# DeltaNet scan, before and after: 16x16 blocks turned on VectorE by 0/1 columns, DRAM scratch laid out by half of the partitions, 15 transfers per pair of steps in place of 36

## The reference, cut to what matters

```python
lmat = jnp.where(strict, jnp.einsum('bhnik,bhnjk->bhnij', k_beta, k) * decay, 0.0)
tmat = triangular_solve(eye + lmat, eye, left_side=True, lower=True, unit_diagonal=True)
u = tmat @ v_beta
w = tmat @ (k_beta * exp(g))
intra = where(incl, (q @ k^T) * decay, 0.0)
def step(S, xs):
    v_new = u_c - w_c @ S
    o_c = q_c @ S + a_c @ v_new
    S = S * exp(gl_c) + k_c^T @ v_new
```

## Time and profile before

| | us |
|---|---|
| median of three runs | 2504.52 |
| the profiled execution: its own time | 2506.25 |
| the profiled execution: its span | 2504.3 |
| PE busy in the span | 2159.4 (86%) |
| DVE, ACT, POOL busy | 906.5, 682.8, 266.2 |
| DMA queue of SP and ACT: share of 16 engines | 20.5% |

### The profile page before, as it was taken

One profiled execution on the slowest core, in us unless ns is written; L12 is line 12 of the kernel. 1 busy time (PEld: TensorE's weight loads), 2 busy tenths in 40 slices (PEclk: granted clock), 3 DMA queues, 4 the chain that ended last, 5 costly groups with the idle time before them and its releaser, 6 DMA issues. The chain is left out here.

```text
span 2504.3 us, 39485 instructions
## 1 busy us (share of the span) xinstructions
PE 2159.4 (86%) x16431; PEld 1329.9 (53%) x16431; DVE 906.5 (36%) x1760; ACT 682.8 (27%) x1386; POOL 266.2 (11%) x381
## 2 busy tenths in 40 slices
PE   4987999989997587888897999999999699799960
PEld 3545676665553477877753555555455444344420
DVE  3254666634883355455551011010223300000116
ACT  6122666643441232332220000000111122122223
POOL 2000000000000444433100000000000000000013
PEclk8998999999998698999898999999999699999985
DMA  9324000010100232323203111120313455776225
GB/s 331 130 88 121 4 4 1 2 43 26 30 0 1 43 63 46 62 43 58 57 0 92 26 34 43 25 67 1 136 60 117 150 185 179 250 239 214 85 101 201
DMA packets 240544, 210.12 MB, mean 84 GB/s; under 512 B 130348, under 2 KB 202352, under 8 KB 239728
## 3 DMA queue, kind: packets, MB, share of 16 engines
q1 hardware_dynamic: 223632, 152.93, 20.5%
q0 software_dynamic: 11696, 36.31, 4.9%
q10 hardware_dynamic: 5040, 18.35, 1.8%
HBM read 165.37 MB, written 42.01 MB: 83 GB/s over the span
## 5 line engine op out<-in xcount | busy, mean ns | idle before, releaser
L741 PE MATMUL ps<-R 128*128 128x512 f32 (+1 forms) x816 | 301.2, 530 | 11.3 <-SPq L525 8.4
L1008 PE MATMUL ps<-R 128*128 128x512 f32 (+1 forms) x768 | 286.1, 526 | 19.9 <-DMA R<-in_w_dn_br_dram 17.8
L1084 PE MATMUL ps<-R 128*128 x560 | 260.1, 619 | 25.7 <-SPq L653 22.5
L900 PE MATMUL ps<-R 64*64 64x64 f32 x5120 | 181.7, 230 | 67.8 <-ACT R L1280 30.5
L741 PEld LDWEIGHTS ps<-R 128*128 128x128 f32 x816 | 158.6, 195 | 150.7 <-issue 132.8
L1008 PEld LDWEIGHTS ps<-R 128*128 128x128 f32 x768 | 147.2, 192 | 152.3 <-issue 144.9
L900 PEld LDWEIGHTS ps<-R 64*64 64x64 f32 x5120 | 172.0, 145 | 87.4 <-ACT R L1280 37.4
L1084 PEld LDWEIGHTS ps<-R 128*128 128x128 f32 x560 | 110.7, 199 | 169.6 <-issue 169.6
L1753 DVE TENSOR_TENSOR R<-ps,R 128x512 f32<-128x512 f32 (+1 forms) x48 | 28.9, 603 | 394.1 <-ACT R L1353 393.3
L1920 DVE COPY R<-ps 128x256 f32<-128x256 f32 x35 | 14.9, 425 | 383.4 <-PE ps L1109 383.4
L2071 POOL DMA_INDIRECT R<-h_scratch,slot_i x35 | 33.0, 942 | 1124.6 <-DVE slot_i L1903 749.6
(11 more groups left out here) (265 smaller groups left out, 2700.0 us busy)
## 6 DMA issues: line engine op xcount, KB each, us to landing
R<-in_w_mod_dram SPq DMA_DIRECT2D x12, 2048.0 KB, 9.1
slot_output<-R ACTq DMA_DIRECT2D x35, 512.0 KB, 3.6
R<-in_w_gate_e_dram SPq DMA_DIRECT2D x16, 1024.0 KB, 6.8
R<-in_w_up_e_dram SPq DMA_DIRECT2D x16, 1024.0 KB, 10.2
R<-in_w_down_e_dram SPq DMA_DIRECT2D x16, 1024.0 KB, 12.0
R<-in_w_in_dram SPq DMA_DIRECT2D x30, 512.0 KB, 5.4
R<-tu_scratch SPq DMA_DIRECT2D x160, 64.0 KB, 2.6
R<-in_x_sample_dram SPq DMA_DIRECT2D x16, 512.0 KB, 6.0
```

The lines of the kernel that those rows point to most:

```text
L741: last = mm(ps[:, u % 4, 0:w], w_sb[n % NW][:, k, :], hT[:, k, c0:c0 + w], start=(k == 0), stop=(k == KD - 1))
L900: last = mm(ps[lo, bank, a * C:(a + 1) * C], lhs(a)[lo], rhs(a)[lo], start=start and (alone or a == 0), stop=stop and (alone or a == PAIRS ...
L1008: mm(ps[:, o + x, 0:w], wk[:, x, k, :], hT[:, k, c0:c0 + w], start=(k == 0), stop=(k == KD - 1))
L1084: last = mm(ps[:, 2 + t % 2, :], hsT[t % 2][:, k, :], R[:, bass.ds(at + (RB + k * 512), 512)], start=(k == 0), stop=(k == KD - 1))
```

## The change

Per pair of steps POOL writes L with 2 transfers a step in place of 4 (both directions in one, 64x8x64). SP reads all 128 blocks with one transfer in place of 4. The scratch `tu_scratch` is laid out so that both directions and two steps lie together; SP writes it with 2 transfers in place of 8 and reads it with 4 a step in place of 8. No byte more or less is moved, and the pieces keep their sizes (64 bytes in the block transfers, 256 bytes in the planes).

Transposing goes from ACT to DVE. A constant `block_dir` has two columns of 0 and 1 that tell by partition which direction a block is of. DVE makes `b_turn = b_in * dir0 + b_in^T * dir1` with two instructions ahead of the substitution, and two more each for the matrix `b_t` (the inverse for direction 0, the transposed one for direction 1) and for `b_u` (the other way) behind it. `b_t` is the buffer `b_in`. The semaphores `bt_turned` and `base_turned` and the two ACT instructions are gone. SP's loop runs over pairs; the context state is stored two pairs later than before, behind the planes of pair 4.

The diff, cut:

```diff
-    parts = [np.eye(P), same, np.ones((P, P))] + upto + after_bd + level + [eye, -eye, rot, before]
+    parts = [np.eye(P), same, np.ones((P, P))] + upto + after_bd + level + [eye, -eye, rot, before, (part[:, None] // 16) % 2 == np.arange(2)[None, :]]
...
-        tu_d = nc.dram_tensor("tu_scratch", [4, 2, P, 16 * PLANE // P], F32).ap()
+        tu_d = nc.dram_tensor("tu_scratch", [2, 4, P, 16 * PLANE // P], F32).ap()
...
-        b_in, b_turn, b_inv, b_invt = [scr(256, "R1").rearrange("p (r c) -> p r c", r=16) for _ in range(4)]
+        b_in, b_turn, b_inv, b_u = [scr(256, "R1").rearrange("p (r c) -> p r c", r=16) for _ in range(4)]
+        b_t = b_in
...
-        def planes_of(x, n, d, h):
-            return bass.AP(x.tensor, (16 * n + 8 * d + 4 * h) * PLANE, [[C, C], [PLANE, 4], [1, C]])
+        def planes_of(x, n, h):
+            return bass.AP(x.tensor, (16 * n + 8 * h) * PLANE, [[C, C], [PLANE, 8], [1, C]])
+
+        def blocks_of(x, n):
+            return bass.AP(x.tensor, 16 * n * PLANE, [[16 * C + 16, P], [C, 16], [1, 16]])
...
             def inverses_back(b):
                 sp.wait_ge(S["base_done"], b + 1)
-                sp.wait_ge(S["base_turned"], b + 1)
                 for s in (2 * b, 2 * b + 1):
                     if s - 4 >= 0:
-                        sp.wait_ge(S[f"tu_in{(s - 4) % 3}"], landed(s - 4, 3, 8))
-                    for d in range(2):
-                        for x in range(2):
-                            src = b_inv if x == d else b_invt
-                            sp.dma_start(blocks_of(tu_d, 2 * (s % 4) + x, d), src[block_rows(s, d)]).then_inc(S["tu_out"], 16)
-                sp.wait_ge(S["tu_out"], 128 * (b + 1))
+                        sp.wait_ge(S[f"tu_in{(s - 4) % 3}"], landed(s - 4, 3, 4))
+                for x, src in enumerate((b_t, b_u)):
+                    sp.dma_start(blocks_of(tu_d, 4 * x + 2 * (b % 2)), src).then_inc(S["tu_out"], 16)
+                sp.wait_ge(S["tu_out"], 32 * (b + 1))
                 for s in (2 * b, 2 * b + 1):
                     if s - 2 > 0:
                         sp.wait_ge(S["vn_mm"], s - 2)
                     for x in range(2):
-                        for d in range(2):
-                            for h in range(2):
-                                sp.dma_start(tu[s % 3][h * C:(h + 1) * C, x, 4 * d:4 * d + 4], planes_of(tu_d, 2 * (s % 4) + x, d, h)).then_inc(S[f"tu_in{s % 3}"], 16)
-
-            for s in range(NCK):
-                sp.wait_ge(S["lt_out"], 64 * (s + 1))
-                if s % 2 == 0 and s > 0:
-                    inverses_back(s // 2 - 1)
-                if s // 2 > 0:
-                    sp.wait_ge(S["base_done"], s // 2)
-                    sp.wait_ge(S["bt_turned"], s // 2)
-                for d in range(2):
-                    sp.dma_start((b_turn, b_in)[d][block_rows(s, d)], blocks_of(lt_d, s, d)).then_inc(S["bt_in"], 16)
-                if s == CTX_CH + 2:
+                        for h in range(2):
+                            sp.dma_start(tu[s % 3][h * C:(h + 1) * C, x], planes_of(tu_d, 4 * x + s % 4, h)).then_inc(S[f"tu_in{s % 3}"], 16)
+
+            for b in range(NCK // 2):
+                sp.wait_ge(S["lt_out"], 64 * (b + 1))
+                if b > 0:
+                    sp.wait_ge(S["base_done"], b)
+                sp.dma_start(b_in, blocks_of(lt_d, 2 * b)).then_inc(S["bt_in"], 16)
+                inverses_back(b)
...
-            inverses_back(NCK // 2 - 1)
...
-                if n >= 2 and n % 2 == 0 and n // 2 - 1 < NCK // 2:
-                    b = n // 2 - 1
-                    act.wait_ge(S["bt_in"], 64 * (b + 1))
-                    if b > 0:
-                        act.wait_ge(S["base_done"], b)
-                    f(b_turn[C:2 * C].rearrange("p r c -> p c r"), b_in[C:2 * C], ACT.Copy).then_inc(S["bt_turned"], 1)
...
-                if n >= 2 and n % 2 == 0 and n // 2 - 1 < NCK // 2:
-                    b = n // 2 - 1
-                    act.wait_ge(S["base_done"], b + 1)
-                    if b > 0:
-                        act.wait_ge(S["tu_out"], 128 * b)
-                    f(b_invt.rearrange("p r c -> p c r"), b_inv, ACT.Copy).then_inc(S["base_turned"], 1)
...
-                signal = "base_done" if i == 15 else "dve_chain"
-                v.tensor_reduce(b_inv[:, i, 0:i], tmp, AX.X, ALU.add, negate=True).then_inc(S[signal], 1)
-                dve.wait_ge(S[signal], count(signal))
+                v.tensor_reduce(b_inv[:, i, 0:i], tmp, AX.X, ALU.add, negate=True).then_inc(S["dve_chain"], 1)
+                dve.wait_ge(S["dve_chain"], count("dve_chain"))
             def base(b, first, end):
                 if first == 1:
-                    dve.wait_ge(S["bt_in"], 64 * (b + 1))
-                    dve.wait_ge(S["bt_turned"], b + 1)
-                    if b > 0:
-                        dve.wait_ge(S["base_turned"], b)
-                        dve.wait_ge(S["tu_out"], 128 * b)
+                    dve.wait_ge(S["bt_in"], 16 * (b + 1))
+                    v.tensor_scalar(b_turn, b_in, block_dir[:, 0:1], None, ALU.mult).then_inc(S["dve_chain"], 1)
+                    dve.wait_ge(S["dve_chain"], count("dve_chain"))
+                    v.scalar_tensor_tensor(b_turn, b_in.rearrange("p r c -> p c r"), block_dir[:, 1:2], b_turn, ALU.mult, ALU.add).then_inc(S["dve_chain"], 1)
+                    dve.wait_ge(S["dve_chain"], count("dve_chain"))
                 for i in range(first, end):
                     substitute(b, i)
+                if end == 16:
+                    if b > 0:
+                        dve.wait_ge(S["tu_out"], 32 * b)
+                    for x, dst in enumerate((b_t, b_u)):
+                        v.tensor_scalar(dst, b_inv, block_dir[:, x:x + 1], None, ALU.mult).then_inc(S["dve_chain"], 1)
+                        dve.wait_ge(S["dve_chain"], count("dve_chain"))
+                        signal = "base_done" if x else "dve_chain"
+                        v.scalar_tensor_tensor(dst, b_inv.rearrange("p r c -> p c r"), block_dir[:, 1 - x:2 - x], dst, ALU.mult, ALU.add).then_inc(S[signal], 1)
+                        dve.wait_ge(S[signal], count(signal))
...
-                        pool.wait_ge(S["lt_out"], 64 * (n - 1))
-                    for d in range(2):
-                        for h in range(2):
-                            pool.dma_start(planes_of(lt_d, n - 1, d, h), la[(n - 1) % RING][h * C:(h + 1) * C, 1, 4 * d:4 * d + 4]).then_inc(S["lt_out"], 16)
+                        pool.wait_ge(S["lt_out"], 32 * (n - 1))
+                    for h in range(2):
+                        pool.dma_start(planes_of(lt_d, n - 1, h), la[(n - 1) % RING][h * C:(h + 1) * C, 1]).then_inc(S["lt_out"], 16)
```

More of the change, by code:

```diff
@@ L129, in build @@
         levels = take(2 * 2 * C).rearrange("p (l d c) -> p l d c", l=2, d=2)
-        eye_st, neg_eye, rot, before = take(C), take(C), take(P), take(P)
+        eye_st, neg_eye, rot, before, block_dir = take(C), take(C), take(P), take(P), take(2)
         small = sb("small", [P, small_np.shape[1]])
@@ L183, in build @@
           ot_used  pad_zeroed
-          gm_ready decay_mm e_ready gr_ready e_masked el_ready kd_ready qd_ready gram_mm la_ready lt_out bt_in bt_turned
-          base_done base_turned tu_out x4_mm x4_ready t4_mm t4_ready u4_mm u4_ready x5_mm x5_ready u5_mm u5_ready
+          gm_ready decay_mm e_ready gr_ready e_masked el_ready kd_ready qd_ready gram_mm la_ready lt_out bt_in
+          base_done tu_out x4_mm x4_ready t4_mm t4_ready u4_mm u4_ready x5_mm x5_ready u5_mm u5_ready
           kt_mm kdec_ready r_mm r_ready vn_mm vn_ready kv_mm s_ready qs_mm av_mm o_used
@@ L556, in inverses_back @@
                     for x in range(2):
[L557 to L570 removed]
+                        for h in range(2):
[6 more added lines that the diff above has]
+                inverses_back(b)
+                if b == CTX_CH:
                     sp.wait_ge(S["s_ready"], PAIRS * CTX_CH)
@@ L912, in _ @@
                 if now:
-                    pe.wait_ge(S[f"tu_in{s % 3}"], landed(s, 3, 8))
+                    pe.wait_ge(S[f"tu_in{s % 3}"], landed(s, 3, 4))
                     pe.wait_ge(S["la_ready"], s + 1)
@@ L1720, in _ @@
                         dve.wait_ge(S["av_mm"], s)
-                        dve.wait_ge(S["lt_out"], 64 * s)
+                        dve.wait_ge(S["lt_out"], 32 * s)
                     v.tensor_tensor(la[n % RING].rearrange("p x a c -> p a x c"), ps[:, 0:2, :].rearrange("p b (a x c) -> p (b a) x c", a=4, x=2),
@@ L1982, in _ @@
                 for x in range(2):
-                    pool.dma_start(tu_d[i, x], zero_f).then_inc(S["pool_dma"], 16)
+                    pool.dma_start(tu_d[x, i], zero_f).then_inc(S["pool_dma"], 16)
             pool.wait_ge(S["pool_dma"], 128)
```

5 lines of the change are left out of this document (removed).

## The result

The changed kernel takes 2488.63 us (median of five runs, 2484.59 to 2492.22), the kernel before 2502.87 beside it: ratio 0.994, 95% interval 0.9927 to 0.9953, 14.2 us less. Run again later beside the kernel before it took 2494.19 against 2501.29 (0.9966, 0.9951 to 0.9982), so its gain lies between 7 and 14 us, where 34.8 were forecast. The time lies in the range that was stated (2452 to 2492), but the sum behind it came out otherwise. All medians here are of executions in the faster of the chip's two states; one of e5's six, with 4598.7 us, was not and is left out.

A forecast was written before the change was run, and what follows sets the result against it. PE was taken to be held in the scan by waits for ACT's copy, `tu` and DVE's mask. Terms 15.4 + 10.1 - 1.7 + 11 = 34.8 us off 2504.52 gave 2470 us, range 2452 to 2492.

The forecast's parts named there:

- What bounds the kernel now: PE waits in the scan: 29.8 us for ACT's copy, 21.7 for planes in `tu`, 14.9 for DVE's mask.
- SP and DMA: Fewer, larger transfers: writing phase 4.9 us, chain 10.6 for 15.7; `tu` waits 15.4 us less, first pair included.
- DVE, added: Turning instructions on DVE per pair: 1.0 us ahead of the first substitution row, 2.0 behind the last.
- odd waits: PE at the head of odd iterations: ACT's copy wait replaced by mask waits; with POOL's share 31.5 us, 1.7 more.
- The term of 0.3 us a pair: POOL's masking beside DVE's last substitution rows and new instructions slows DVE: 2.7 us in all.
- Late substitutions: SP free earlier for the next L, so the 14.9 us of mask waits go, less 4.8: 10.1 us gained.
- even waits: PE's waits in even iterations for the mask before `u5`, 14.9 us: forecast to fall by 10.1.
- The first substitution rows: 1.0 us more before the `x5` mask, cover just used up; 4.8 us of waits stick out.
- The clock: PE's slow stretches after four `tu` waits and two long mask waits go: 11 us come back.
- The rivals: Chain fits partly, 2491 (0.13); issues not the limit, 2504 (0.07); slower transfers, 2545 (0.05); more gained, below 2456 (0.09).
- the 2 us of the first pair: `tu` wait before the first pair: chain gains 5.1 us, new DVE instructions lose 3.0, 2 us net.

The follow-up runs named there:

- e5: The changed kernel with DVE's turning behind the substitution done twice over, 2.0 us more of DVE per pair: 2522.5 us.
- e9: The kernel before, 36 transfers, with ACT's turning behind the substitution moved behind the v_new copy and the decay exponentials: 2510.1 us.
- e1: The changed kernel with POOL's two writes of L issued first in its iteration, ahead of its kd and qd products: 2490.4 us.
- e3: The changed kernel without its six turning operations per pair, transfers left as they are: 2439.9 us.
- e8: The kernel before with SP's reads of L and writes of the blocks merged over the pair, 30 transfers, ACT turning: 2493.4 us.
- e14: The changed kernel without the two turning operations ahead of the substitution, the four behind it kept: 2480.7 us.
- e7: The kernel before with DVE turning as in the change, planes and 36 transfers as they were: 2523.2 us.
- e10: The kernel before with 18 transfers per pair through another order of the planes, ACT turning as before: 2481.4 us.
- e12: The kernel before with 18 transfers, ACT's turning moved behind the v_new copy and exponentials, and POOL writing L first: 2473.8 us.

## Why the prediction was wrong, point by point

**What bounds the kernel now** named the three places rightly, and e9 shows what it missed: they are one loop with two paths, DVE's string and the chain over DRAM, of nearly one length with 36 transfers. Taking 3 us off one only hands the wait to the other.

**SP and DMA**: right. 4.67 us of writing for 4.9, the chain 10.1 us (998.32 to 1003.02 + 3 x 0.755 + 3.1, the median landing of a read) for 10.6, and the waits for `tu` behind the first pair 1.7 us and, in the second profile, 0, where there were 13.5. Only the first pair fails: 9.5 us for 8.3, where I had it 2 us better. SP's first write there comes 3.9 us later than before, behind 3.4 us of turning, and the chain behind it is 4.4 us shorter; `x4` starts 0.5 us earlier, and PE had come to it 1.8 us earlier than before.

**DVE, added**: right for the pair alone (0.35 and 0.65 us, 1.04 together), low behind the substitution: 2.57 us for 2.0 from 995.75 on, since the first instruction stands beside POOL's (0.83 for 0.35). The odd waits came out at 34.2 us for 31.5, 2.7 more. The block between DVE and POOL is larger than the 0.4 of the earlier trace rows: 0.68 and 0.80 in e1. The term of 0.3 us a pair for it, 2.7 in all, was too small: with the six operations DVE is busy 237.1 us in the scan and without them 201.4 (e3), 35.7 more, where their own lengths (0.35 and 0.65) make 27. The other 9 us, 1.0 a pair, are instructions that took longer, and those seen to do so stand beside POOL's.

**The failed step is "Late substitutions"**: it said that SP is free in time, that DVE never waits for L and that 10.1 us are gained in the even iterations. The even waits rose instead, from 14.9 us to 21.1 (18.8 in the second profile), and DVE waited for L eight times, 10.4 us. That step asked when SP is free, not when both halves of L are written; POOL's L2023 at 1012.54 sets it, and the merged read, which could be issued only at the later of two events, moved from 3.8 to 5.1 us behind the `x4` products of its iteration. e1 shows it by taking it away (10.4 -> 0.3, even waits 21.1 -> 8.4), e8 by bringing it without DVE's turning (14.9 -> 22.5). The turning ahead, forecast in *The first substitution rows* at 4.8 us of waits, is worth 12.6 by e14 (21.1 -> 8.5): with the cover of 1.0 us gone it stands wholly before the mask. Taking away either of the two, the late write (e1) or the turning ahead (e14), takes some 12.6 us off the even waits, so their sizes don't add up. The term was -10.1 us and measured +6.2 (+3.9 in the second profile), 16.3 us (14.0) on the wrong side.

**The clock**: what failed is what the term hung on. I reckoned 11 us for waits that fall by 23.8 (15.4 + 10.1 - 1.7), 0.46 us per us. In the table PE's busy time goes from 318.5 at 70.5 us of waits (e7) to 296.3 at 22.9 (e3), 0.47 per us, and a straight line through all seventeen rows gives 0.41. But the waits in the scan fell by 1.2 to 5.5 us only, and the busy time by 3.0 to 4.4. Nor does every wait have this price: e14 has 9.8 us less of waits than the second profile of the changed kernel (14.1 less than the first): the even ones are shorter, the odd ones stay at 3.7 to 3.9 us each, and PE's busy time is 0.5 us more (1.9). That a gap of 3.5 us (3.2 and 0.3) would stand in front of every odd iteration was in my own sum.

By the terms, in the scan: `tu` -11.7 us for -13.4, odd waits +4.4 for +1.7, even waits +6.2 for -10.1, clock -4.4 for -11. That is -5.5 us by the profile of the first run (its scan: -5.7). The second profile gives -13.4, +4.1, +3.9 and -3.0, -8.4 in all (its scan: -8.7), and the medians -7.1 and -14.2. The forecast was -34.8, with the 2 us of the first pair. That 2488.6 lies within the range all the same is due to its width, not to the mechanism.

**The rivals**: none of them was this. All asked whether the transfers are cheap; they are. By e7 and the changed kernel the transfers gain 29 to 35 us where DVE turns, and DVE's turning costs 23.1 of them (e7 against before); where ACT turns they gain 20.5 (e10). A rival with the turning as the new bound was wanted, and I had the number for it, 3 us a pair.

## What to carry to other kernels

Where PE waits by turns for an engine and for a chain through DRAM, write down each path's length per round: the shorter one has only the difference to give, and work put on the longer one costs its length and often the clock besides (here, by e3, 34.1 us of waits came with 13.6 us of PE's busy time). Before an engine takes work over from another, ask whether it has an idle place between the two things that others wait for, not what its busy share is: DVE was busy 36% of the span, and the six operations still cost 46 to 54 us. And a merged transfer starts with the latest of its parts, so look up who writes the last part and what stands before it in that engine's queue.

## What the runs showed of the hardware that was not expected

- A DVE instruction beside POOL's products was 0.14 to 0.80 us longer (128x16 in 0.73 us for 0.19, 128x121 in 1.06 for 0.38, 128x225 in 1.35 for 0.55), long rows as much as short ones. It ends just behind POOL's: L1656 at 996.58 where POOL's L2027 (995.11, 1.31 us) ends at 996.42. The Trainium skill (SBUF — State Buffer, "Who interferes with whom") says that a DVE instruction with two SBUF inputs contends with a POOL instruction that reads SBUF, that one in a 2-port mode contends too, and that whoever comes second is blocked for the whole instruction. These rows agree, and the 0.3 us a pair that I took instead was too little. POOL's order is therefore part of DVE's time: 11.4 us of it in e12 for two writes of L moved.
- Issuing hardly grows with the number of pieces: two writes of 128 KB in pieces of 64 bytes are issued in 1.27 to 1.36 us, 0.64 to 0.68 each, where eight of 32 KB took 4.0 to 5.3, 0.50 to 0.67 each: four times the pieces for some 0.1 us more. They land later: 3.9 us in the median for 1.9 by the earlier trace rows; reads of 128 KB in 3.1 for 2.6.
- Through TensorE's clock a wait cost more than its length in this scan: over the runs of the table, with 22.9 to 74.1 us of waits, PE's busy time rose by 0.4 to 0.5 us per us of waits. e14 is the exception: fewer waits, the same busy time.
